# A two-layer trunk on one core: the first two weight slabs on unscaled turned rows, input slab first

## What is computed

```
h = einsum('bsd,de->bse', rms_norm(x, ev_norm), w_in)
aq, af, ai, bq, bk, bv, z = split(h)
oa = hgrn2_chunked(heads(aq), heads(af), heads(ai), lb)   # af through a sigmoid: forget gates
y = concatenate([head_norm(oa), moba_attention(...)]) * silu(z)
x = x + einsum('bse,ed->bsd', y, w_out)
```

## Time and profile before

| | us |
|---|---|
| three runs | 583.30, 583.51, 583.58 |
| median | 583.51 |
| the profiled execution | 583.43 |
| its span in the trace | 581.6 |
| PE busy | 572.6 (98%) |
| DVE, ACT, POOL busy | 432.9, 392.1, 73.0 |

### The profile page before, as it was taken

The page is one execution under the profiler, slowest core; times in us unless marked ns, Lnnn a source line. Parts: engine busy times, 40 slices in busy tenths (PEclk is TensorE's granted clock), DMA queues, the critical chain, the costliest instruction groups (busy, mean ns, idle before and its releaser), DMA issues.

```text
span 581.6 us, 9044 instructions
## 1 busy us (share of the span) xinstructions
PE 572.6 (98%) x3492; PEld 511.4 (88%) x3492; DVE 432.9 (74%) x675; ACT 392.1 (67%) x600; POOL 73.0 (13%) x77
## 2 busy tenths in 40 slices
PE   8999999999999999999999999999999999999995
PEld 7999989899899888888888889999889988888985
DVE  6879689687766874567766896799998974876663
ACT  6864784578458575657666858969759837566764
POOL 4230005036401000100000001102110200100002
PEclk9999999999999999999999999999999999999998
DMA  9856355556824834564344545336544563356201
GB/s 297 255 179 225 101 189 192 172 159 174 238 82 149 286 145 144 169 231 181 144 145 155 207 150 192 122 118 222 212 147 146 172 233 140 116 209 228 97 1 73
DMA packets 51854, 98.84 MB, mean 170 GB/s; under 512 B 1732, under 2 KB 7140, under 8 KB 51812
## 3 DMA queue, kind: packets, MB, share of 16 engines
q1 hardware_dynamic: 50628, 96.95, 49.2%
q0 software_dynamic: 1024, 1.05, 0.8%
q10 hardware_dynamic: 160, 0.27, 0.1%
HBM read 96.16 MB, written 1.05 MB: 167 GB/s over the span
## 4 chain that ended last, share of the span: by engine, by line
PE 97%; DVE 1%; DMA 1%; ACT 1%; issue 0%; DVEq 0%; SPq 0%; ACTq 0%
PE proj L1951 14%; PE proj L1976 10%; PE proj L1975 10%; PE proj L1977 10%; PE proj L1934 9%; PE proj L1936 9%; PE proj L1935 9%; PE proj L1952 7%; PE head L2191 4%; PE proj L1956 2%; PE head L2269 1%; PE proj L1955 1%; PE head L2035 1%; DMA x_residual<-in_x_dram 1%; PE head L2168 1%; PE head L2236 1%
## 5 line engine op out<-in xcount | busy, mean ns | idle before, releaser
L1166 DVE TENSOR_TENSOR w_lo<-raw_weights,w_hi 128x1024 fp32r<-128x1024 f32 x174 | 223.9, 1300 | 91.2 <-ACT w_hi L544 88.3
L544 ACT ACTIVATE w_hi<-raw_weights 128x1024 fp32r<-128x1024 f32 x174 | 182.3, 1056 | 108.7 <-PE proj L1977 49.6
L1934 PE MATMUL proj<-xT,w_hi 128*128 128x256 f32 x432 | 123.7, 286 | 0.0
L1936 PE MATMUL proj<-xT,w_lo 128*128 128x256 f32 x432 | 122.2, 283 | 0.0
L1935 PE MATMUL proj<-xT,w_hi 128*128 128x256 f32 x432 | 122.2, 283 | 0.0
L1951 PE MATMUL proj<-xT,w_hi 128*128 128x512 f32 x280 | 101.6, 402 | 0.0
L1934 PEld LDWEIGHTS proj<-xT,w_hi 128*128 128x128 f32 x432 | 82.8, 192 | 0.8 <-DVEq L1218 0.4
L1935 PEld LDWEIGHTS proj<-xT,w_hi 128*128 128x128 f32 x432 | 82.8, 192 | 0.3
L1936 PEld LDWEIGHTS proj<-xT,w_lo 128*128 128x128 f32 x432 | 82.8, 192 | 0.0
L1952 PE MATMUL proj<-xT,w_lo 128*128 128x256 f32 x280 | 78.4, 280 | 0.0
L1975 PE MATMUL proj<-w_hi,y 128*128 128x512 f32 x176 | 69.4, 394 | 0.0
(11 more groups left out here) (327 smaller groups left out, 899.1 us busy)
## 6 DMA issues: line engine op xcount, KB each, us to landing
raw_weights<-in_ev_w_in_dram SPq DMA_DIRECT2D x15, 2048.0 KB, 9.2
raw_weights<-in_od_w_in_dram SPq DMA_DIRECT2D x12, 2048.0 KB, 8.1
raw_weights<-in_ev_w_out_dram SPq DMA_DIRECT2D x4, 2048.0 KB, 7.7
raw_weights<-in_xa_wkv_dram SPq DMA_DIRECT2D x4, 2048.0 KB, 8.3
raw_weights<-in_od_w_out_dram SPq DMA_DIRECT2D x4, 2048.0 KB, 7.7
raw_weights<-in_xa_wq_dram SPq DMA_DIRECT2D x2, 2048.0 KB, 9.1
raw_weights<-in_xa_wo_dram SPq DMA_DIRECT2D x2, 2048.0 KB, 8.0
x_residual<-in_x_dram SPq DMA_DIRECT2D x2, 512.0 KB, 4.0
```

The costliest lines, as they stand in the source:

```text
L544: act.activation(ring_quarter(w_hi, n, q), raw_quarter(n, q), ACT.Copy).then_inc(hi_ready, 1)
L1166: dve.tensor_tensor(ring_quarter(w_lo, n, q), raw_quarter(n, q), ring_quarter(w_hi, n, q).bitcast(F32), ALU.subtract).then_inc(lo_ready, 1)
L1934: pe.matmul(dst, wh[:, k, :], x_hi[:, k, :], start=(k == 0), stop=False)
L1936: last = pe.matmul(dst, wl[:, k, :], x_hi[:, k, :], start=False, stop=(k == KC - 1))
```

## The change

Slab 0 is now the input slab of group 0 (kind T), slab 1 the forget slab. PE turns x as it lands, without the row factor. ACT and DVE multiply by the gain and split the turned rows into `y_hi` and `y_lo`. Slabs 0 and 1 are multiplied with these. The row factor comes in later: per token, so as a scale in ACT's copy of the input slab to `v_sb`; and for the forget slab, whose tokens lie along the free dimension, as a product with `row_factors`, which PE makes with two small matmuls of a matrix of ones with a diagonal (`factor_diag`) and ACT copies. `scaled_logits` on DVE does that product before the sigmoid. For all later slabs DVE forms the normed rows from the turned ones (`normed_rows`, eight of 128x256), ACT rounds them (`normed_high`), DVE takes the low part (`normed_low`, two of 128x1024). Slab 0 is loaded in six transfers by rows, slab 1 in four by columns, before the later parameters. In stage A (g = 0) the `ahead` calls stand elsewhere. In cross attention 0 one query sum moves ahead of one `ahead`.

```diff
-for _g in range(2):
-    SLABS += [("A", "f", "F", _g), ("A", "i", "T", _g), ("A", "q", "F", _g), ("A", "z", "X", _g)]
+SLABS += [("A", "i", "T", 0), ("A", "f", "F", 0), ("A", "q", "F", 0), ("A", "z", "X", 0)]
+SLABS += [("A", "f", "F", 1), ("A", "i", "T", 1), ("A", "q", "F", 1), ("A", "z", "X", 1)]
...
+            for c, (k, n_k) in enumerate(((0, 1), (1, 1), (2, 1), (3, 1), (4, 2), (6, 2))):
+                sp.dma_start(raw[:, 0, :].rearrange("p (k c) -> p k c", k=KC)[:, k:k + n_k, :],
+                             dram_slab(0)[:, k:k + n_k, :]).then_inc(first_landed[c], 16)
...
+            for q in range(4):
+                sp.dma_start(raw_quarter(1, q), dram_slab(1)[:, :, P * q:P * q + P]).then_inc(second_landed[q], 16)
...
+            for k in range(2):
+                pool.wait_ge(first_landed[k], 16)
+                pool.tensor_copy(first_rows(w_hi, k), raw_quarter(0, 0)[:, k, :])
+                pool.drain().then_inc(first_hi[k], 1)
             pool.tensor_tensor(ring_quarter(w_lo, 0, 0), raw_quarter(0, 0), ring_quarter(w_hi, 0, 0).bitcast(F32),
+                               ALU.subtract).then_inc(first_lo[0], 1)
...
+            raw_high(range(0, 6))
             row_squares(1, 1024)
...
+            raw_high(range(6, 8))
             ahead(-1, 3)
+            act.wait_ge(factors_psum, 1)
+            act.activation(row_factors, proj[3][:, 0:S], ACT.Copy).then_inc(factors_ready, 1)
...
+            raw_low(range(0, 4))
+            first_high(2)
+            raw_low(range(4, 6))
+            first_high(3)
+            dve.drain()
+            dve.tensor_tensor(ring_quarter(w_lo, 0, 1), raw_quarter(0, 1), ring_quarter(w_hi, 0, 1).bitcast(F32),
+                              ALU.subtract).then_inc(first_lo[1], 1)
             row_factor(1)
...
+            dve.wait_ge(factors_ready, 1)
+            normed_rows([0, 1])
+            ahead(i0, 0)
...
+            def scaled_logits(n, u):
+
+                filled(dve, n, u)
+                dve.tensor_tensor(blocks(0)[:, 2 * u:2 * u + 2, :], bank(n, u).rearrange("p (h t) -> p h t", h=2),
+                                  row_factors.rearrange("p (a t) -> p a t", a=1).broadcast_to([P, 2, S]), ALU.mult
+                                  ).then_inc(f_scaled, 1)
+                dve.drain().then_inc(free_of(n, u), 1)
...
+                else:
+                    scaled_logits(f, 0)
+                    ahead(f, 1)
+                    forget(g, 0)
+                    ahead(f, 2)
+                    ahead(f, 3)
+                    scaled_logits(f, 1)
...
-            pe.wait_ge(row_normed, 1)
-            tile_turned(0, 0)
...
+            for t in range(T):
+                pe.wait_ge(x_landed[t], 16)
+                for b in range(4):
+                    tile_turned(t, b)
...
+                    first_slab(i)
+                    pe.wait_ge(prm_ready, 1)
+                    slab_f(f, [0, 1], x=(y_hi, y_lo))
...
-                ahead(nv, 0)
                 query_summed(nq, 3)
+                ahead(nv, 0)
```

More of the change, by code:

```diff
@@ L184, in hybrid_trunk @@
         trig_ready = sem("trig_ready")
-        first_lo = sem("first_lo")
+        first_lo = [sem(f"first_lo{q}") for q in range(2)]
         eps_filled = sem("eps_filled")
@@ L631, in _, with raw_high, normed_high @@
             act.preload_act_table(ACT.Sqrt)
+            def raw_high(ks):
+                for k in ks:
+                    if k < 4:
+                        act.wait_ge(turned, k + 1)
+                    else:
+                        act.wait_ge(raw_lo_ready, k - 3)
+                    act.activation(y_hi[:, k, :], turned_at(k), ACT.Copy, scale=param("ev_norm", k)
+                                   ).then_inc(raw_hi_ready, 1)
+            def normed_high(j):
+                act.wait_ge(rows_normed, j + 1)
+                act.activation(xT_hi[:, 4 * j:4 * j + 4, :], x_normed[:, 4 * j:4 * j + 4, :], ACT.Copy
+                               ).then_inc(xT_hi_ready, 4)
             row_squares(0, 512)
@@ L696, in stage_a @@
                     rstd_a(0)
-                ahead(i, 2)
-                ahead(i, 3)
+                    ahead(i, 2)
+                    ahead(i, 3)
+                else:
+                    ahead(q, 0)
+                    act.wait_ge(prm_turned, 3)
+                    act.activation(prm[:, N_EARLY:], head[0][:, N_EARLY:N_ROWS], ACT.Copy).then_inc(prm_ready, 1)
+                    ahead(q, 1)
                 act.wait_ge(b_ready, g + 1)
@@ L1301, in _ @@
             dve.drain()
+            normed_low(1)
+            ahead(slab("A", "f", 0), 0)
             def angles():
@@ L1392, in stage_a @@
                     sign_trig()
-                ahead(f, 1)
-                ahead(f, 2)
-                forget(g, 0)
-                ahead(f, 3)
-                ahead(i, 0)
+                    ahead(f, 1)
+                    ahead(f, 2)
+                    forget(g, 0)
+                    ahead(f, 3)
+                    ahead(i, 0)
+                else:
+                    scaled_logits(f, 0)
+                    ahead(f, 1)
+                    forget(g, 0)
+                    ahead(f, 2)
+                    ahead(f, 3)
+                    scaled_logits(f, 1)
                 forget(g, 1)
@@ L1418, in stage_a @@
                     gated_a(0)
[L1419 removed]
+                    ahead(i, 3)
+                else:
+                    ahead(q, 0)
+                    ahead(q, 1)
                 dve.wait_ge(exps_ready, 3 * g + 3)
                 dve.tensor_tensor(wview(0), wview(1), wview(0), ALU.mult).then_inc(kinv_ready, 1)
[L1422 to L1423 removed]
+                if g:
+                    ahead(q, 0)
+                    ahead(q, 1)
                 ahead(q, 2)
@@ L2094, in second_quarter_products @@
-            def second_quarter_products(n):
-                pe.wait_ge(hi_ready, 2)
-                dst = bank(n, 0)[:, S:2 * S]
-                wh, wl = ring_quarter(w_hi, n, 1), ring_quarter(w_lo, n, 1)
-                for k in range(KC):
-                    pe.matmul(dst, wh[:, k, :], xT_hi[:, k, :], start=(k == 0), stop=False)
-                    pe.matmul(dst, wh[:, k, :], xT_lo[:, k, :], start=False, stop=False)
-                pe.wait_ge(lo_ready, 2)
-                for k in range(KC):
-                    last = pe.matmul(dst, wl[:, k, :], xT_hi[:, k, :], start=False, stop=(k == KC - 1))
-                last.then_inc(quarter_used, 1)
```

233 lines of the change are left out of this document (124 added, 109 removed).

## The result

The changed kernel takes 586.15 us (585.92 to 587.53, 6 runs), the kernel before 583.51 (6 runs): a ratio of 1.0046, interval 1.0033 to 1.0058. It is slower, by 2.6 us; the forecast was 583.9 and a range up to 585.3. The profiled execution took 586.15 us with a span of 584.4 (583.43 and 581.6 before).

The account below looks back on a forecast made before the run. PE was taken to bound the kernel (97% of the chain of waits). 583.43 + 0.5 (s2q3) + 0.05 (qdec) + 0.3 (lock at s3q2) - 0.46 (query sum) = 583.8, so 583.9 us as median; range 581.8 to 585.3.

Parts of the forecast that it names:

- The mechanism that it named: Fourth query quarter: DVE falls behind, its low part behind the scan comes late, and PE gets a new 1.1 us wait.
- The start: PE's first product comes at 8.2 us instead of 9.72, 1.5 us sooner.
- The lock itself: First slab: DVE's cast for chunk 2 waits for POOL's whole subtraction, through shared ports; PE waits 0.6 us.
- The first slab: Input slab: PE waits 0.6 us at chunk 2, starts s0q2 at 15.4 and the forget slab at 21.0.
- DVE's stretch: DVE works without a gap from 15.5 us for 18.4 us, so the second `scaled_logits` starts at 33.9.
- Slab 2: Its transfer, issued at 17 to 19 us, lands by 27.5; its first quarter is due on ACT at about 28.5.
- rival (c): Slab 2's transfer lands late; a landing at 29.5 us costs 1 us, 584.9; chance 0.06.
- L2168 and the lock at s3q2: Keys and queries: a tie of DVE and PE costs 0.05 us, POOL's product possibly delaying DVE's s3q2 0.3.
- "No further wait" at the mask copies: DVE runs some 2.5 us later up to the copies; the last comes at about 61, PE asks at 62.
- The query sum: Cross attention 0: the sum runs before a low part, so score 3 loses its wait; gain 0.46 us.
- Rival (b): POOL and DVE collide more often, in the mask stretch (0.6 us) and at s3q2 (0.8): 585.3; chance 0.17.
- Rival (a): DVE keeps up and the wait at s2q3 vanishes: 581.9 us; chance 0.27.

Follow-up runs that it names:

- changed_again: The changed kernel run once more, unedited, to look at the start; 585.95 us, with the kernel before at 583.47.
- heads_wait: The changed kernel without PE's wait for all four mask copies, each head waiting for its own copy; 585.16 us, kernel before 583.76.
- casts_on_pool: The changed kernel with the first four weight casts all on POOL and both first subtractions on DVE; 585.63 us, kernel before 583.49.
- all_split_angles: Changed kernel: per-head copy waits, casts on POOL, parameter steps shared, query work reordered, slab 2 issued earlier, no second warm-up, angles split behind mask copies; 581.88 us.
- quarter_in_log: The changed kernel with the fourth query quarter split early, DVE's low part during ACT's logarithm; 586.07 us, kernel before 583.49.

## Why the prediction was wrong

The mechanism that it named decides, at the place that it named; the steps failed by size, and one by a wrong count.

- **The start** (PE at 8.2; chunk 2 at 10.6). In the profiled run PE began at 9.03, since it still turned rows at the slow step; in five others it began at 8.15 to 8.3 and in the rest at 7.8 to 9.1, so 8.2 was fair. But it doesn't matter: what counts is POOL's subtraction, which I had from 7.8 to 10.2 and which ran from 8.17 to 10.55, with the cast's end 0.28 behind. I had taken the landing of the first 256 KB at 6.4; the cast on it began at 6.58 and those of other runs at 6.21 to 7.30. The lock itself was right: in `changed_again`, where PE began at 8.27, it waited 0.7 at chunk 2.
- **The first slab.** s0q2 at 16.02 instead of 15.4, the forget slab at 21.86 instead of 21.0, the third query quarter 1.1 later than I had it. So the 0.6 us that I had as slack ahead of the fourth query quarter is a delay of 0.48.
- **DVE's stretch** (18.4 us from 15.5 to 33.9) is the term with the largest error. It ran from 16.12 to 35.41, 19.3 us: 0.6 late at its start, 0.3 more for eight scaled rows (3.4), 0.5 more for the parameter chain (3.0), 0.1 for the rest. The 0.5 is an idle time of DVE in the middle of that chain (0.50 ahead of L1376), where I had it "without a gap". The profile names no releaser for it, and it stands in every trace of the changed kernel and its edits that leaves this chain on DVE, one to three steps later where fewer DVE instructions stand ahead of it; its cause is open. The eight and two low parts were right (9.1 and 2.3), and so was the chain behind (42.88 - 35.41 = 7.47 for 7.5). PE got the quarter at 44.25 instead of 42.8: a wait of 1.4 for 1.1, and in all +1.9 instead of +0.5.
- I also had DVE's sum as the only bound of that stretch. By the traces it is one of three that end together at 24 to 25.6 us.
- **Slab 2** landed at 29.02, 9.8 us after its issue at 19.18, and not by 27.5; ACT waited 1.89 for it, the sign that I had named for rival (c). It cost nothing by itself: the sigmoid behind it ended at 32.04, and DVE reached the first forget pair at 32.49.
- **L2168 and the lock at s3q2** (0.35 in the sum): 0.13. DVE came first and POOL waited, 2.07 us for its product of 1.07.
- **"No further wait" at the mask copies** was a wrong step. I had the last copy at 61; the copies begin at 61.18 and end at 63.18, because DVE was 4.6 us behind the kernel before by then (56.59), not 2.5, and PE's code waits there for all four. Of the 2.1 us that I had too few, 1.25 stood already at L1537 (50.09 for 46.34 is 3.75). The other 0.85 is one collision behind it: DVE's product L1540 took 1.54 for 0.69, and ended 0.55 behind POOL's L481, which ran from 50.14 to 51.68. From there to the copies DVE has no idle time. Price 0.83, and `heads_wait` gives it back whole.
- **The query sum** 0.46: 0.5 to 0.53. Right.

The sum by these: 583.8, + 1.4 at the quarter, - 0.2 at L2168, + 0.8 at the readout, + 0.35 at the end of the program (with the column transfers) gives 586.15. I had nothing for the last two. Rival (b), slower by collisions, had a like time (585.3) and, at other places than it named, a part of the cause. The stretched cast was in my sum already; without it (`casts_on_pool`) PE's delay at the readout is 0.7 less. The stretched L1540 was not: an estimate from the rows puts the copies' end at 63.18 - 0.85 = 62.33 without it, and PE came to them at 60.41 + 2.04 = 62.45, so the wait at the readout would be gone. No run takes this collision alone away. Rival (a) needed DVE to keep up; it takes the edits of `all_split_angles` for that.

## What to carry to other kernels

When a change brings a long chain of small steps closer to the product that needs it, count the whole queue of the engine that carries it, past the first wait too: the lateness came back at the readout 19 us later, where the kernel before had had 1.8 us of slack, with one collision of DVE and POOL on top. Swapping two entries of such a queue only moved the wait (`quarter_in_log`), and taking away one cause gave back at most 0.8 us of the 2.6; here it took five edits together to draw level, and the angles, which could wait longest, had to go behind what PE waits for to get ahead. Where two engines shut each other out, look at who stands behind the stretched operation in its own queue, even if that is 10 us away. And where one wait stands for several producers, ask whether each consumer needs only its own.

## What the runs showed of the hardware

- A POOL memset that reads nothing held a DVE cast just as a subtraction does: it ran from 11.88 to 13.69 us, and the cast beside it ended at 13.96 (2.35 us for 0.61). The cast's row starts at 11.61, ahead of the memset's and inside a cast of POOL (11.44 to 11.95), so here a DVE operation that waited for one POOL instruction waited for the next one too. The Trainium skill (SBUF — State Buffer, "SBUF: two separate sides") has the lock for DVE operations in a two-port mode against any GpSimd one, and the trace agrees. In the other direction POOL's pair of 0.73 took 2.60 beside two DVE subtractions. Two products with both inputs in SBUF shut each other out too: DVE's L1540 took 1.53 or 1.54 beside POOL's, and 0.68 or 0.69 without it, in all the traces of the changed kernel and its edits.
- Four column transfers of a slab (512-byte pieces) kept SP's queue for 7.55 us, the same slab in whole rows 0.40 (though the parameter transfer behind it then took 1.62). The traces with the column transfers also end 0.32 to 0.38 us later behind the last output transfer.
- TensorE's 128-column passes at the start go from a step of 0.21 us to 0.11 at a moment between 4.4 and 7.0 us that differs between runs of the same program (6.9 and 5.4 in the two traces of the changed kernel), while the granted clock reads 1.00 (the upper level) all the time.

```profile
11.88 1.81 POOL L442 MEMSET work<- 128x2048 f32 x1
```

```profile
10.43 2.60 POOL L436 TENSOR_SCALAR_AFFINE_SELECT seen_f<-seen_f 128x128 f32<-128x128 f32 x2 [0.17 <-issue]
```
